# Two residual blocks on one core: six places in the hand-written order of VectorE, ScalarE and GpSimd are changed

## What is computed

```python
# first block
h = rmsnorm(x, norm_mix_g);  proj = h @ w_in           # 9 x 1024 columns and 16 more
y_a = short_conv_branch(bg, cg, xv, conv_a_w) @ w_a_out
y_b = gdn_branch(q, k, v, z, a, b, ...) @ w_b_out      # 8 heads, gated delta rule in chunks
x = x + (sigmoid(ga) * y_a + sigmoid(gb) * y_b) @ w_o
h = rmsnorm(x, norm_ffn_g)
up = causal_dwconv(h @ w_up, conv_w); gate, val = split(up)   # 2 x 2816 columns
x = x + (silu(gate) * val) @ w_down;  x = rmsnorm(x, norm_final_g)
# second block
h = rmsnorm(x, norm_g_2); z = h @ w_in_2               # split into pool, DSA, FoX parts
a_out = pool_mixer(pv) * silu(pg)                      # windows of 2, 4, 8, 16 tokens
b_out = dsa_mixer(dq, dk, dv, iq, ik, iw, 128) * silu(dg)   # 6 heads over the top 128 keys
c_out = fox_mixer(fq, fk, fv, log_f) * silu(fg)        # 6 heads, decay sums F added to the scores
x = x + concat(a_out, b_out, c_out) @ w_out_2;  out = rmsnorm(x, final_g_2)
```

## Time and profile before

| | |
|---|---|
| median of 3 runs | 1307.31 us |
| the profiled execution, its own time | 1307.49 us |
| its span, first to last instruction | 1305.8 us |
| TensorE matmul busy | 1287.5 us, 99% |
| TensorE weight load busy | 1029.0 us, 79% |
| VectorE busy | 824.9 us, 63% |
| ScalarE busy | 560.7 us, 43% |
| GpSimd busy | 258.9 us, 20% |
| chain of work that ended last | PE 91%, DVE 5%, issue 1%, ACT 1% |

### The profile page before, as it was taken

The page is one execution under the profiler, slowest core; times in us unless marked ns, Lnnn a source line. Parts: engine busy times, 40 slices in busy tenths (PEclk is TensorE's granted clock), DMA queues, the critical chain, the costliest instruction groups (busy, mean ns, idle before and its releaser), DMA issues.

```text
span 1305.8 us, 20307 instructions
## 1 busy us (share of the span) xinstructions
PE 1287.5 (99%) x6833; PEld 1029.0 (79%) x6833; DVE 824.9 (63%) x1685; ACT 560.7 (43%) x1010; POOL 258.9 (20%) x500
## 2 busy tenths in 40 slices
PE   8999999999999999999999999999999999999998
PEld 6877878878888788888888888888887776767786
DVE  6976667676676753445477773377755688895823
ACT  5654535445454532223344442244444454445422
POOL 2513303032130400001300000000022234455310
PEclk9999999999999999999999999999999999999999
DMA  6323222232332223333233323433233333222221
GB/s 184 90 66 90 80 82 78 80 83 72 86 88 64 80 81 97 96 96 97 81 102 99 98 75 97 120 93 96 72 93 103 93 113 86 66 65 65 65 65 65
DMA packets 210052, 114.44 MB, mean 88 GB/s; under 512 B 7696, under 2 KB 206671, under 8 KB 210005
## 3 DMA queue, kind: packets, MB, share of 16 engines
q1 hardware_dynamic: 210005, 113.84, 30.1%
HBM read 111.70 MB, written 2.13 MB: 87 GB/s over the span
## 4 chain that ended last, share of the span: by engine, by line
PE 91%; DVE 5%; issue 1%; ACT 1%; DMA 0%; DVEq 0%; SPq 0%; POOLq 0%; ACTq 0%; POOL 0%
PE gb L679 77%; PE gb L1158 2%; PE gd L1158 1%; PE gd L1086 1%; PE gd L1109 1%; PE gd L1099 1%; PE gd L787 1%; PE gd L879 1%; PE gd L870 1%; DVE wlo L1645 1%; PE gd L775 0%; PE gd L858 0%; PE gd L859 0%; PE gd L691 0%; PE gd L875 0%
## 5 line engine op out<-in xcount | busy, mean ns | idle before, releaser
L679 PE MATMUL gb<-act_a,whi 128*128 128x512 f32 x2656 | 898.1, 400 | 0.6 <-DVE wlo L1645 0.6
L679 PEld LDWEIGHTS gb<-act_a,whi 128*128 128x128 f32 x2656 | 499.0, 188 | 118.1 <-issue 15.5
L679 PE MATMUL gb<-act_a,wlo 128*128 128x512 f32 x1416 | 552.3, 390 | 0.0
L1645 DVE TENSOR_TENSOR wlo<-raw,whi 128x1024 fp32r<-128x1024 f32 (+2 forms) x189 | 226.5, 1199 | 147.7 <-ACT whi L1190 145.7
L1190 ACT ACTIVATE whi<-raw 128x1024 fp32r<-128x1024 f32 (+1 forms) x211 | 217.2, 1029 | 232.4 <-PE gb L679 201.9
L679 PEld LDWEIGHTS gb<-act_a,wlo 128*128 128x128 f32 x1416 | 266.7, 188 | 48.1 <-issue 1.0
L679 PE MATMUL gb<-act_b,whi 128*128 128x512 f32 x432 | 152.5, 393 | 0.1
L679 PEld LDWEIGHTS gb<-act_b,whi 128*128 128x128 f32 x432 | 81.1, 188 | 17.6 <-DVE qc L1922 0.5
L2467 POOL TENSOR_TENSOR zs<-zs,ca 128x512 f32<-128x512 f32 x3 | 4.2, 1397 | 322.3 <-ACT ca L1193 322.3
L2512 POOL TENSOR_TENSOR wlo<-raw,whi 128x1024 fp32r<-128x1024 f32 x22 | 52.8, 2401 | 57.5 <-ACT whi L1190 57.5
L679 PE MATMUL gb<-act_b,wlo 128*128 128x512 f32 x128 | 49.9, 390 | 0.0
(11 more groups left out here) (508 smaller groups left out, 1586.1 us busy)
## 6 DMA issues: line engine op xcount, KB each, us to landing
raw<-in_w_in_dram SPq DMA_DIRECT2D x102, 512.0 KB, 3.4
raw<-in_w_up_dram SPq DMA_DIRECT2D x44, 512.0 KB, 3.6
raw<-in_w_down_dram SPq DMA_DIRECT2D x16, 384.0 KB, 3.1
raw<-in_w_down_dram SPq DMA_DIRECT2D x16, 320.0 KB, 3.0
raw<-in_w_a_out_dram SPq DMA_DIRECT2D x8, 512.0 KB, 3.4
raw<-in_w_b_out_dram SPq DMA_DIRECT2D x8, 512.0 KB, 3.4
raw<-in_w_o_dram SPq DMA_DIRECT2D x8, 512.0 KB, 3.4
raw<-in_w_out_dram SPq DMA_DIRECT2D x8, 512.0 KB, 3.5
```

Source lines behind the costliest of these rows:

```text
L679: ins = pe.matmul(gb[:, b, :], l, r, start=(first and m == 0), stop=(last and m == len(todo) - 1))
L1645: dve.tensor_tensor(wlo[:, i % 2, 0:k * P], raw[:, i % 4, 0:k * P], whi[:, i % 2, 0:k * P].bitcast(F32), ALU.subtract).then_inc(split_read ...
```

## The change

- **Gates' tanh.** In ScalarE's walk over the 31 units, the tanh of a gate unit is issued behind quarter 1's pieces of work for every gate unit, and not only in the one unit where group 0 begins.
- **Weighings.** The two `weigh` of a pair stand in the same slot, start + 4n + 3. Before, the second one stood in the next.
- **Residual products.** GpSimd's eight products of `xT` run beside units 22 to 29, before beside 19 to 26.
- **Four orders in the first head and around it.** ScalarE's `level(15)` goes ahead of `filter_first` and `norm_hi(5)`. On VectorE `taps(h)` goes behind `step(20, h - 1)`; `ya_low` leaves the end of its own head and goes behind the `step` of quarter (0, 1) of the next; behind the last head, behind the first `step` of the units of `w_a_out`.
- **Last up unit.** The last turn of the second up loop is written out on ScalarE and VectorE, and `split` of down unit 2 stands inside it: on ScalarE ahead of the wait for the last product of gate and value, on VectorE ahead of the last low part.
- **Decay sums.** VectorE's `cum_f` goes ahead of `z_out` in its quarter.

```diff
-                todo.setdefault(start + 4 * n + 3 + t % 2, []).append((5, ("weigh", c, t)))
+                todo.setdefault(start + 4 * n + 3, []).append((5, ("weigh", c, t)))
...
                 level(14)
+                level(15)
                 filter_first()
                 norm_hi(5)
-                level(15)
                 split(N_B + 8, N_B + 8)
...
-                with sc.Fori(0, FF_CUT[f] // 2) as i:
+                def up_turn(i, last=False):
...
                             else:
+                                if last and q == 1:
+                                    split(N_DN[1] + 2, N_DN[1] + 2, FF_CUT[1] // 2)
                                 sc.wait_ge(up_ready, j + 1)
...
+                with sc.Fori(0, FF_CUT[f] // 2 - f) as i:
+                    up_turn(i)
+                if f == 1:
+                    up_turn(FF_CUT[1] // 2 - 1, last=True)
...
-                        for n in ((2, 3, 4), (5,))[j] if j < 2 else range(2 * j + 2, min(2 * j + 4, 2 * KD + 1)):
+                        for n in ((3, 4), (5,))[j] if j < 2 else range(2 * j + 2, min(2 * j + 4, 2 * KD + 1)):
...
-                    if m == 1 and u and u != GROUP_AT // 4:
+                    gate_next = u and Z_UNITS[u - 1][0] in ("g", "pg")
+                    if m == 1 and u and not gate_next:
                         z_out(u - 1)
                     for e in plan.get((u, m), ()):
                         beside(e)
-                    if m == 1 and u == GROUP_AT // 4:
+                    if m == 1 and gate_next:
                         z_out(u - 1)
...
                 rescale(7)
-                ya_low(0)
 
             def head(h):
-                taps(h)
...
+                        if (s, m) == (0, 0):
+                            taps(h)
+                        if (s, m) == (0, 1):
+                            ya_low(h - 1)
...
-                        if (s, m) == (7, 3):
-                            ya_low(h)
...
                         step(20 + j * 4 + m, HEADS - 1)
+                        if (j, m) == (0, 0):
+                            ya_low(HEADS - 1)
...
                                 dve.tensor_tensor(g[:], g[:], dst[:], ALU.mult).then_inc(up_ready, 1)
+                                if last and q == 1:
+                                    split(N_DN[1] + 2, N_DN[1] + 2, FF_CUT[1] // 2)
                                 dve.wait_ge(up_hi, j + 1)
...
-                    if not (crossed and q == 1):
+                    if not crossed:
                         split(N_DN[f] + 4 * i + 2 * q + 2, N_DN[f] + 2 * q + 2, next_k)
...
+                    early = [e for e in plan.get((u, m), ()) if e[0] == "cum_f"]
+                    for e in early:
+                        beside(e)
                     if m == 1 and u:
                         z_out(u - 1)
                     for e in plan.get((u, m), ()):
-                        beside(e)
+                        if e not in early:
+                            beside(e)
...
-                k = n - (N_Z + 19)
+                k = n - (N_Z + 22)
                 if 0 <= k < KD:
                     pool.tensor_tensor(xT[:, k, :], xT[:, k, :], final_row, ALU.mult).then_inc(xT_norm, 1)
```

More of the change, by code:

```diff
@@ L2109, in _, with up_turn @@
             for f in range(2):
-                with dve.Fori(0, FF_CUT[f] // 2) as i:
-                    own.enter(i, 4)
+                def up_turn(i, last=False):
                     for q in range(2):
@@ L2136, in _ @@
                                                   ALU.subtract).then_inc(up_lo, 1)
-                own.leave(FF_CUT[f] // 2)
+                with dve.Fori(0, FF_CUT[f] // 2 - f) as i:
+                    own.enter(i, 4)
+                    up_turn(i)
+                own.leave(FF_CUT[f] // 2 - f)
+                if f == 1:
+                    up_turn(FF_CUT[1] // 2 - 1, last=True)
                 kh = FF_CUT[f] // 2
```

## The result

The changed kernel takes 1310.3 us, the median of 8 runs (1308.64 to 1312.58); the kernel before takes 1307.4 us in the same comparison. The ratio is 1.0021 (95% interval 1.0012 to 1.0030). The forecast was 1304.5 us, with a range up to 1307.4, so by the medians the change costs 2.9 us where 2.8 were expected back; by the lowest runs (1308.64 against 1307.23) it costs 1.4. The profiled execution of the changed kernel took 1308.93 us with a span of 1307.2.

The account below looks back on a forecast made before the run. TensorE, busy 1287.5 of 1305.8 us, bounds the kernel, so only its late starts can be won. Gains 0.52 + 0.4 + 1.26 + 0.5 + 0.1 = 2.78 us gave 1304.7 profiled, 1304.5 as median; range 1302.4 to 1307.4.

Parts of the forecast that it names:

- GpSimd's products where they go: Units 27 to 29, beside the pool's windows: delays up to 0.7 us hide; cost 0, bounds 0 and 3.1.
- What bounds the kernel, and where the stalls go: TensorE's timeline: late starts at seven places, 6.85 us together, belong to the change's parts; the loop over heads has none.
- the last paragraph: Signs to look for in the new profile, among them line 858 at 76.7 as before and `qc` about 0.7 late.
- Last up unit: TensorE at 954.31 no longer waits for down unit 2's `wlo`: gain 0.52 us, lower bound 0.2.
- Decay sums: At 1036.78 the copy comes before TensorE gets there, without `z_out` ahead: gain 0.4 us, between 0.32 and 0.48.
- Gates' tanh: At 1090.00 the 2.0 us stall goes and 0.7 reappears at `qc`: gain 1.26 us, bounds 0.7 and 2.0.
- First head: Stalls at 68.46 and 76.77, 0.91 and 0.59 us, are taken over by `Rr`: gain 0.1, from 0 to 0.6.
- Weighings and products: From 1127 to 1175 us VectorE bounds; shorter `Yb` weighing returns 0.84, part lost to a split: gain 0.5, between 0 and 2.35.
- Rival A: Moved GpSimd products hold up the pool's windows, making TensorE late at 1224.85: costs 0.5 to 3.1 us, 1306.5; chance 0.22.
- Rival C: Second weighing blocks the next pair's scores: 1.4 us per pair met, four of 24 pairs, 1310.1 us; chance 0.06.
- the forecast for the profiled execution: Whole kernel: the profiled 1307.49 us less the summed gain of 2.78, giving 1304.7 us.

Follow-up runs that it names:

- tanh alone: The kernel before with only the change to the gates' tanh on ScalarE: lowest 1306.50, median 1306.72 us, ratio 0.9987.
- first four experiments: Runs of the changed kernel again, and of it with the second weighing, GpSimd's products, or both undone: medians 1310.14, 1309.39, 1307.79 and 1305.70 us.
- second weighing back: The changed kernel with the second weighing of a pair in the next quarter again: lowest 1307.87, median 1309.39 us, ratio 1.0005.
- products back: The changed kernel with GpSimd's eight products beside units 19 to 26 again: lowest 1306.80, median 1307.79 us, ratio 0.9996.
- products in other units: The changed kernel with the second weighing in the next quarter and GpSimd's products in units 19, 20, 22 to 26 and 30: median 1304.75 us, ratio 0.9973.
- both back: The changed kernel with both the second weighing and GpSimd's eight products where they were before: lowest 1305.56, median 1305.70 us, ratio 0.9980.
- product 28 elsewhere: The changed kernel with the second weighing in the next quarter and GpSimd's products beside units 22 to 27, 29 and 30: median 1306.48 us, ratio 0.9990.
- first head, up unit, decay sums: The kernel before with only the first head's orders, the last up unit and the decay sums changed: lowest 1306.15, median 1307.75 us, ratio 0.9994.
- all groups but 0: The changed kernel with GpSimd's products beside units 19 to 26, and group 0's second weighing in the next quarter: median 1306.68 us, ratio 0.9989.
- both back, one MAX8 more: The changed kernel with second weighing and products undone, and one VectorE MAX8 done twice in one round: lowest 1306.11, median 1306.74 us, ratio 0.9992.

## Why the prediction was wrong, point by point

The step that failed is "GpSimd's products where they go", with "cost 0", and beside it the nothing that stands in the sum for the second weighing outside its own stretch. In their place the runs showed 3.1 us late near 1227 with the products alone moved (2.31 by the lowest runs, after the 0.83 gained before), and 1.3 near 1068 for the second weighing (1.24 by the lowest runs).

**What bounds the kernel, and where the stalls go: right but for one.** The stalls of 68, 954, 1036, 1090, 1163 and 1166 went. The one of 76.77 did not: TensorE gets there earlier by the gain at 68, and waits 0.69 for `S`, before 0.59. The step on the first head said that it goes, the last paragraph that it stays. `Rr` (0.28 late), `qc` near 1093 and one of the turns behind the pair took over, as written.

**Last up unit: right.** 0.52 late before, none after. The split of VectorE stands at 951.74 (0.82) and the low part at 952.53.

**Decay sums: right.** 0.4 forecast, 0.40 measured (0.72 between the starts before, 0.32 after); the copy is over at 1035.35.

**Gates' tanh: mechanism right, size 0.2 to 0.3 too high.** With the weighings together `qc` is 0.95 late where 0.7 was forecast (gain 1.05 in place of 1.26); with the tanh alone `zs` (0.54) and `qc` (0.52) are late (gain 0.95).

**First head: 0.1 forecast, 0.2 measured, and given back elsewhere.** The late starts go from 1.4 (line 842 0.82, line 858 0.59) to 1.20 (line 849 0.23, line 858 0.69, line 870 0.28). The prediction counted 0.91 for line 842, because it took the undisturbed spacing as 0.23 where it is 0.32. The first up unit, near 653, is 0.60 late in place of 0.39 in every kernel that has the edits of the first head and the up loop, and not in the one with the tanh alone. VectorE's first read there begins 0.58 us behind the end of ScalarE's `Vt`, before 0.21. Which edit does it was not tried.

**Weighings and products: wrong, and here the forecast fell.** The step put a gain of 0.5 on the stretch at 1127 to 1175, and nothing on the rest. In the stretch itself the weighing of `Yb` did take 0.35, not 1.19, but the chain then ran into the two operations that GpSimd holds next (they were held before too: 1.72 for line 2231 at 1169.51, 1.26 for `qc` at 1171.34). Timeline of DVE of the changed kernel:

```profile
1161.18 0.35 DVE L2273 TENSOR_SCALAR Yb<-Yb,small 128x256 f32<-128x256 f32 x1
1167.85 1.90 DVE L2248 TENSOR_SCALAR selb<-selb 128x512 f32<-128x512 f32 x1
1169.85 1.23 DVE L2273 TENSOR_SCALAR qc<-qc,small 128x384 f32<-128x384 f32 x1
```

`qc` is 2.11 late against 0.66, 1.70 and 0.38 before with 0.41 for `kc`, so 1.0 came back there, and 0.4 of it went to `Yb` near 1178. What is left, 0.6, is about the 0.5 of the step. What failed is the nothing that it put beside it. For the products the step read two margins, and took the second weighing's move to give room in units 27 to 29. It gave none: before, the weighing of `kc` at 1215.04 stood through the split (2.18 us), and after the change line 2343 stood there in its place (2.62). Line 2345 then ended 4.1 us behind the start of that split, before 3.3, and the weighing of `zs` that now goes first added 0.26. So the copy of 128x2, which began 0.84 us ahead of the next split before (1222.98 against 1223.82), began 0.18 behind it.

**Rival A happened, but not on the path it named.** It had the mechanism (line 2343 waits as the low part did), the place, and bounds of 0.5 to 3.1; the stall is 2.94 in the changed kernel. It had `Yb` and then the pair behind it weighed late at 1224.85, but both weighings took 0.35 and were in time. That 2.94 lies inside its bounds is luck in part. I gave it 0.22, because the margins were 0.1 us, and this was the fault: with a margin of 0.1 us in a chain which the same change moves by more than that, the case in which nothing is held had no more right than the other. The price was also put into the wrong operation. For the delay of lines 2343 and 2345 itself nobody waits; it costs by what it pushes. The copy of 0.16 us that slipped behind the split carried 2.2 of the stall, and the sum behind the copy 1.0.

By the rule that the prediction quoted from the Trainium skill, SBUF — State Buffer, section Who interferes with whom, the windows had to wait, and the runs agree for line 2343 (2.62 us) and line 2345 (1.14). The same section says that copy, cast and tensor_scalar can also contend, in a mode that uses both ports; the copy of 128x2 (2.37), the one of 128x4 (1.26) and the weighings (1.51, 2.17), which are tensor_scalar, agree in that they are held, and the prediction had left these copies out. A copy of 128x1 is not held: it takes 0.15 at 1209.70 in the changed kernel, beside the product at 1208.74. Which mode an operation ran in no trace shows.

**Rival C happened once.** It asked 1.4 us for each pair met and four pairs. One pair was met, behind a GpSimd step of 1.34 us and not behind a split, and it cost 1.3. What the rivals left out is that they do not exclude each other, nor the forecast: the forecast for the profiled execution, the stall of A and one pair of C, with the sizes that were measured, are 1304.7 plus 2.9 plus 1.3, that is 1308.9, against 1308.93 measured. That the two agree so closely is luck: the 0.2 too much for the tanh and the 0.2 lost near 653 are hidden in it by smaller terms. As chances of one out of four cases, this sum stood nowhere, and so the range ended at 1307.4.

**The clock: not in the forecast at all.** The other 1.4 us up to the median of 1310.3 are told below.

## What to carry to other kernels

Where VectorE and GpSimd hold each other up, an operation's price is set by the one it meets, and 0.2 us decided here whether it took 0.16 or 2.37 us: write down for every GpSimd instruction that is moved which VectorE operations start within its length and who waits for them, and price each margin below the shift of the change itself as open. An order that costs 1.3 us in one group (weighing, weighing, maxima in group 0) costs nothing in others, and seems to help in group 3 once no product stands beside it, so a schedule's rule is better given by group than for all. And rivals that can happen together are to be added up before the range is written.

## What the runs showed of the hardware: a long wait of TensorE costs twice

The times of one kernel lie at two levels or more. Of 32 runs of the kernel before beside the first four experiments, 17 lie at 1307.39 to 1307.74 with a granted clock of 0.998 to 1.000 over the whole span, most others at 1308.9 to 1309.3 with 0.997 or 0.998. A profile of the changed kernel that fell on a higher level (1311.52 us) shows where. Windows of that run (us, then busy us and count of PE, PEld, DVE, ACT and POOL, then the granted clock, DMA share and GB/s):

```profile
1170.00:1171.50 1.50, 0.20 (x2) 0.20 (x3) 1.48 (x3) 0.00 (x0) 1.03 (x1) 1.00 0.45 89
1171.50:1173.00 1.50, 1.50 (x8) 1.22 (x7) 1.50 (x5) 0.62 (x2) 0.00 (x0) 0.74 0.88 260
1173.00:1175.00 2.00, 2.00 (x8) 1.60 (x7) 0.49 (x2) 1.67 (x7) 0.00 (x0) 0.50 0.00 0
...
1230.00:1231.00 1.00, 0.16 (x1) 0.19 (x2) 0.93 (x3) 0.69 (x3) 0.00 (x0) 0.63 0.00 0
1231.00:1232.00 1.00, 1.00 (x5) 1.00 (x5) 0.90 (x4) 0.04 (x1) 0.00 (x0) 0.50 0.00 0
```

The same stretch of the first profile, at full clock, does 14 products where this one does 8:

```profile
1173.00:1175.00 2.00, 2.00 (x14) 1.46 (x12) 0.32 (x2) 2.00 (x8) 0.00 (x0) 1.00 0.02 4
```

Behind the wait for `qc` (2.11), and towards the end of that near 1230 (3.00), the granted clock falls to 0.50, that is 1.2 GHz, and the products follow each other every 0.43 us in place of 0.23:

```profile
1172.92 0.63 PE L679 MATMUL gb<-act_a,wlo 128*128 128x512 f32 x1
1173.35 0.63 PE L679 MATMUL gb<-act_a,whi 128*128 128x512 f32 x1
```

The Trainium skill, TensorE: Matmul & The Clock Gate, section What's actually happening, says that the lower level is TensorE's default and that activity releases it; these windows agree as far as they go.

Two more profiles fell on a higher level, and each has one fall, behind the longest wait of its kernel: with the second weighing back behind the 3.12 of `zs` (0.50 from 1228 to 1230), and with the products back behind the 2.27 of `qc`:

```profile
1173.50:1174.50 1.00, 1.00 (x3) 0.76 (x3) 0.99 (x4) 0.70 (x3) 0.00 (x0) 0.50 0.32 94
```

The other eleven profiles have no such stretch between head and tail.

What a fall costs can be read by laying the two profiles of the changed kernel beside each other. The turn of `qc` starts 0.17 later in the slower one (1171.30 against 1171.13). Two later places, first in the faster and then in the slower one:

```profile
1174.72 0.49 PE L1086 MATMUL gd<-gate 64*128 64x128 f32 x4
1178.42 0.66 PE L1099 MATMUL gd<-ident,Yb 128*128 128x128 f32 x4 [0.24 <-DVE Yb L2273]
...
1176.46 0.49 PE L1086 MATMUL gd<-gate 64*128 64x128 f32 x4
1179.75 0.60 PE L1099 MATMUL gd<-ident,Yb 128*128 128x128 f32 x4
```

The scores start 1.74 later, so the fall took 1.6 us. The turn of `Yb` starts only 1.33 later: it was 0.40 late at full clock, and a TensorE that comes 1.6 us later has nothing to wait for. So the fall costs 1.2 net.

Whether it falls differs from run to run of one kernel. The longest late start and the runs with a higher level, kernel by kernel:

| kernel | longest late start | runs higher | by |
|---|---|---|---|
| products in other units | 1.58 | 0 of 8 | |
| tanh alone | 1.69 | 0 of 11 (one at 1307.37 with a clock of 1.000) | |
| both back | 1.71 | 0 of 11 | |
| product 28 elsewhere | 1.80 | 0 of 11 | |
| before (three sets) | 2.01 | 35 of 84 | 1.5 |
| first head, up unit, decay sums | 2.01 | 6 of 11 | 1.5 |
| products back | 2.28 | 7 of 11 | 1.1 |
| all groups but 0 | 2.29 | 7 of 11 | 1.2 |
| both back, one MAX8 more | 2.43 | 6 of 11 | 0.7 |
| second weighing back | 3.12 | 7 of 11 | 1.5 |
| changed | 2.94 and 2.11 | at least 6 of 11 | 1.0 to 3.7 |

The pair that differs by one MAX8 alone is the test: 0.7 us of VectorE in front of one turn brought 0.6 at the lowest, and 1.0 at the median. No profile of that kernel fell on its higher level, so the place of its fall was not seen. The tanh alone takes the kernel before's only wait over 1.80 away, and its higher runs with it, so that it gains 0.7 at the lowest and 2.1 at the median of its set (1308.82 against 1306.72). A median over such runs is no price of an edit: the kernel before had medians of 1307.40 to 1308.82 in four sets of runs. That is why the steps above go by the lowest times and by late starts. The height of the level fits the reading above, 1.6 less the late starts that follow closely. Nothing follows the waits of 2.01 and 3.12 (1.5 and 1.5); `Yb` with 0.40 follows that for `qc` in the kernels with products back and with all groups but 0 (1.1 and 1.2); and `qc` with 0.34 and `kc` with 0.42 follow that for `zs` in the kernel with one MAX8 more, an estimate of 0.8 against 0.7. Why the clock falls in one run of a kernel and not in the next stays open.
